# Early sums of the second output projection, angle tables in pieces, and latent value products that alternate between heads

## The reference

```python
mix_out = sliding_window_attention(q, shared_k, shared_v, swa_sinks[bl])
mem_o = memory_attention(mem_q, mem_k, mem_v)
x = x + jnp.concatenate([mix_out, mem_o], axis=-1) @ w_out[layer]
x = x + swiglu(rms_norm(x, ln_ffn[layer]), w_gate_up[layer], w_down[layer])
```

## Time and profile before

| what | value |
| --- | --- |
| median of 3 runs | 2076.44 us (2074.3 to 2078.44) |
| profiled execution, its own time | 2073.64 us |
| its span, from first to last instruction | 2071.8 us |
| TensorE matmul busy | 1925.9 us, 93% |
| VectorE busy | 1059.4 us, 51% |
| ScalarE busy | 780.4 us, 38% |
| mean granted TensorE clock | 0.962 of full speed |

### The profile page before, as it was taken

How to read it: one execution, slowest core, us unless ns; L and a number is a source line. 1 busy time by engine, 2 the same in 40 slices (tenths; PEclk the granted TensorE clock), 3 DMA queues, 4 the chain that set the end, 5 groups by cost and what they waited for, 6 DMA issues and landing times.

```text
span 2071.8 us, 25534 instructions
## 1 busy us (share of the span) xinstructions
PE 1925.9 (93%) x9978; PEld 1498.0 (72%) x9978; DVE 1059.4 (51%) x1979; ACT 780.4 (38%) x1637; POOL 116.5 (6%) x85
## 2 busy tenths in 40 slices
PE   7999988898987769999988999999999899999997
PEld 5665567685554457788887888788876688888886
DVE  6757556441211157785555543644567654444344
ACT  4455744531111145533543321222346543222222
POOL 0000000000000034020420000000000000000000
PEclk9999999999999959999999999999999999999998
DMA  5101413359999942121001222232221022222221
GB/s 190 39 10 53 145 54 112 142 206 405 413 412 408 405 188 72 62 68 65 1 1 59 96 94 102 73 111 97 96 82 41 30 84 102 102 92 92 102 92 41
DMA packets 76791, 261.07 MB, mean 126 GB/s; under 512 B 7776, under 2 KB 10080, under 8 KB 76288
## 3 DMA queue, kind: packets, MB, share of 16 engines
q1 hardware_dynamic: 66512, 231.46, 30.6%
q0 software_dynamic: 5040, 19.58, 2.8%
q10 hardware_dynamic: 5120, 8.39, 1.1%
HBM read 242.62 MB, written 16.79 MB: 125 GB/s over the span
## 4 chain that ended last, share of the span: by engine, by line
PE 72%; DVE 7%; DMA 6%; ACT 3%; issue 1%; POOL 0%; ACTq 0%; DVEq 0%; SPq 0%; POOLq 0%
PE ps_pair L285 17%; PE ps_pair L286 17%; PE ps_pair L287 17%; DMA split_acts_as_f<-w_experts 4%; PE ps_pair L1995 4%; PE ps_turn L2560 2%; PE ps_pair L2560 1%; PE ps_pair L880 1%; PE ps_out L908 1%; DMA w_places<-w_experts 1%; PE ps_shared L2006 1%; PE ps_out L2006 1%; PE ps_turn L892 1%; ACT g L3347 1%; PE ps_out L2326 1%
## 5 line engine op out<-in xcount | busy, mean ns | idle before, releaser
L285 PE MATMUL ps_pair<-split_acts,w_high 128*128 128x512 f32 (+1 forms) x1816 | 721.3, 397 | 22.7 <-DVE split_acts L614 10.0
L287 PE MATMUL ps_pair<-split_acts,w_low 128*128 128x512 f32 (+1 forms) x1816 | 705.3, 388 | 0.0
L286 PE MATMUL ps_pair<-split_acts,w_high 128*128 128x512 f32 (+1 forms) x1800 | 699.2, 388 | 0.0
L242 DVE TENSOR_TENSOR w_low<-w_raw,w_high 128x1024 fp32r<-128x1024 f32 (+4 forms) x249 | 281.9, 1132 | 269.8 <-ACT w_high L236 268.1
L285 PEld LDWEIGHTS ps_pair<-split_acts,w_high 128*128 128x128 f32 x1816 | 343.7, 189 | 103.2 <-issue 23.3
L287 PEld LDWEIGHTS ps_pair<-split_acts,w_low 128*128 128x128 f32 x1816 | 343.6, 189 | 72.0
L286 PEld LDWEIGHTS ps_pair<-split_acts,w_high 128*128 128x128 f32 x1800 | 341.6, 190 | 67.4 <-issue 1.7
L236 ACT ACTIVATE w_high<-w_raw 128x1024 fp32r<-128x1024 f32 (+4 forms) x249 | 242.8, 976 | 147.1 <-PE ps_pair L287 143.2
L360 DVE TENSOR_TENSOR x<-x,ps_pair 128x512 f32<-128x512 f32 x80 | 54.9, 686 | 147.6 <-PE ps_pair L287 147.6
L2237 DVE TENSOR_TENSOR g<-g,ps_pair 64x256 f32<-64x256 f32 x31 | 13.2, 425 | 197.3 <-ACT g L2177 197.3
L3108 ACT ACTIVATE split_acts<-h 128x512 fp32r<-128x512 f32 x44 | 27.8, 633 | 192.4 <-DVE h L3121 192.4
(11 more groups left out here) (528 smaller groups left out, 2453.4 us busy)
## 6 DMA issues: line engine op xcount, KB each, us to landing
w_raw<-w_gu SPq DMA_DIRECT2D x88, 512.0 KB, 3.4
split_acts_as_f<-w_experts SPq DMA_DIRECT2D x42, 1024.0 KB, 21.2
w_places<-w_experts SPq DMA_DIRECT2D x35, 1024.0 KB, 20.6
w_raw<-w_down SPq DMA_DIRECT2D x32, 448.0 KB, 3.2
w_raw<-w_gdnin SPq DMA_DIRECT2D x26, 512.0 KB, 3.5
w_raw<-w_out SPq DMA_DIRECT2D x24, 512.0 KB, 3.5
x<-w_experts SPq DMA_DIRECT2D x12, 1024.0 KB, 20.1
rows_y<-scratch ACTq DMA_DIRECT2D x64, 128.0 KB, 6.1
```

The source lines that it names most:

```text
L242: dve.tensor_tensor(WL[:, t % SPLIT, 0:kt * m], WRAW[:, t % RING, 0:kt * m], WH[:, t % SPLIT, 0:kt * m].bitcast(F32), ALU.subtract).then_i ...
L285: pe.matmul(out, wh[:, k, :], self.high(k), start=(n == 0), stop=False)
L286: pe.matmul(out, wh[:, k, :], self.low(k), start=False, stop=False)
L287: last = pe.matmul(out, wl[:, k, :], self.high(k), start=False, stop=(n == self.kt - 1))
```

## The change

It does three things.

1. `out1.early(j, n0, n1)` issues steps `n0` to `n1` (input tiles in `OUT_ORDER`) of output tile `j` before the stage itself. Tiles 0 and 1 are begun between the gaps 14 to 18: 4 steps of each, then 2 of each, then 1 of each; 7 of 8 steps of both tiles are then done when `out1` begins. It waits for each input tile with `heads_ready`, now for tile 1 too.
2. The work of the two rope tables is spread over tiles 0 to 9 of `gu01` on VectorE, and the two sine functions go to tiles 5 and 11 on ScalarE.
3. `pe_values` of `Attention` issues the value products of the heads that close together in turn: first product of head `h`, first of head `h+1`, second of head `h`, and so on. Each head is reported after its last product. Only the latent attention has groups that close two heads.

```diff
+            def early(self, j, n0, n1):
+
+                def tensor(pe):
+                    self.tensor_steps(pe, j, n0, n1)
+                    self.begun[j] = n1
+                return On(tensor=tensor)
+
             def tensor_tile(self, pe, j):
-                while scores_read:
-                    need(pe, *scores_read.pop())
+                self.tensor_steps(pe, j, self.begun.get(j, 0), self.kt)
+                if j == 0 and self.opening:
+                    self.opening.tensor_spread(pe)
+
+            def tensor_steps(self, pe, j, n0, n1):
                 t = self.base + j
-                pe.wait_ge(low_ready, t + 1)
-                if t >= BANKS:
-                    wait_evac(pe, t - BANKS)
+                if n0 == 0:
+                    while scores_read:
+                        need(pe, *scores_read.pop())
+                    pe.wait_ge(low_ready, t + 1)
+                    if t >= BANKS:
+                        wait_evac(pe, t - BANKS)
...
-                for n, k in enumerate(self.order):
+                for n in range(n0, n1):
+                    k = self.order[n]
                     if j == 0 and self.ready is not None:
                         need(pe, *self.ready(k))
-                    if j == 0 and self.each is not None:
+                    if (j == 0 or j in self.begun) and self.each is not None:
                         self.each(pe, k)
...
-                    rows, plan_ = self.pv(h)
-                    for lhs, (slot, src, q0, q1), first, lastk in plan_:
+                plans = [(h, *self.pv(h)) for h in closes]
+                for n_part in range(len(plans[0][2]) if plans else 0):
+                    for h, rows, plan_ in plans:
+                        lhs, (slot, src, q0, q1), first, lastk = plan_[n_part]
+                        o = self.o0 + h // self.per_tile
                         last = pe.matmul(self.outs[o % len(self.outs)][rows, q0:q1], lhs,
                                          self.turned[h % len(self.turned)][:, slot, src:src + q1 - q0],
                                          start=first, stop=lastk, skip_group_check=True)
-                    done(last, "att_pe", ("values", self.h0 + h))
+                        if n_part == len(plan_) - 1:
+                            done(last, "att_pe", ("values", self.h0 + h))
...
-        swiglu(0, n_ff0, n_kv, hi, lo, {2: [angles_s.part(0)], 8: [angles_s.part(1)]})
+        swa_angles = {0: [On(vector=angles_s.angles)], 6: [On(vector=angles_s.signed)]}
+        for n, at_ in ((0, 1), (1, 7)):
+            for j, step_of in enumerate((angles_s.turned, angles_s.reduced, angles_s.wrapped)):
+                swa_angles[at_ + j] = [On(vector=lambda dve, n=n, step_of=step_of: step_of(dve, n))]
+            swa_angles[at_ + 4] = [On(scalar=lambda act, n=n: angles_s.part_scalar(act, n))]
+        swiglu(0, n_ff0, n_kv, hi, lo, swa_angles)
...
-        fl += [heads.gap(n) for n in range(len(gaps), N_PAIRED + 3)]
...
-        fl += [Linear("out1", hi2, lo2, None, n_ff1.take_act, n_ff1.take_dve, order=OUT_ORDER, each=heads_ready),
-               n_ff1.rest()]
+        out1 = Linear("out1", hi2, lo2, None, n_ff1.take_act, n_ff1.take_dve, order=OUT_ORDER, each=heads_ready)
+        fl += [out1.early(0, 0, 4), heads.gap(14), out1.early(1, 0, 4), heads.gap(15), out1.early(0, 4, 6),
+               heads.gap(16), out1.early(1, 4, 6), heads.gap(17), out1.early(0, 6, 7), out1.early(1, 6, 7),
+               heads.gap(18), out1, n_ff1.rest()]
```

More of the change, by code:

```diff
@@ L260, in __init__ @@
                 self.base = BASE[name]
-                self.order, self.each = order or range(self.kt), each
+                self.order, self.each, self.begun = order or range(self.kt), each, {}
             def tensor(self, pe):
@@ L294, in tensor_tile @@
                             stage.tensor(pe)
-                if j == 0 and self.opening:
-                    self.opening.tensor_spread(pe)
             def scalar(self, act):
```

## The result

The changed kernel takes 2062.89 us (median of 4 runs, 2062.15 to 2064.12); the kernel before, in runs on the same chip, 2075.59 us (4 runs, 2074.3 to 2078.44). The ratio is 0.9934, with an interval of 0.9922 to 0.9945. 2061.0 was predicted, in a range of 2056 to 2068. A further measurement beside 17 runs of the kernel before gave 2062.9 us and 0.9928 (0.9914 to 0.9942). The profiled execution took 2064.12 us, its span is 2062.3. The medians differ by 12.7 us; the ratio makes it 13.7, anywhere from 11.4 to 16.2.

What follows compares the result with a forecast made beforehand. The prediction took TensorE, busy 93% of the span, as the bound. Its terms -3.1 - 5.6 - 6.7 = -15.4 us, made against the median 2076.44, gave 2061.0 us, range 2056 to 2068.

Steps and rivals of the forecast that it cites:

- Angles, -3.1: In `gu01`, spreading the angle work removes two TensorE holes of 1.55 us each: -3.1 us, bounds -2.0 and -3.1.
- Early sums, -6.7: From the last rotation into `out1`, 42 products moved earlier: -6.7 us after a clock allowance, bounds 0 and -8.5.
- so the stage gains 7.5 us: Tail and start of `out1`: 9.5 us of products moved, 2.0 given back, before the clock allowance.
- the 0.8 us set aside for that: At the restart of `out1`: half of the 1.6 us that 8 products at the lower clock would cost.
- The sign of failure that the prediction names for the tail: The prediction is wrong if the last half's values end over 2 us later than before, counted from the last rotation.
- Alternating values, -5.6: At the four latent value pairs, alternating halves run side by side: -5.6 us in all, bounds 0 and -6.3.
- a block becomes 2.29 us: Each latent pair's value block shrinks from 3.86 to 2.29 us, a gain of 1.57 us.
- the allowances for pairs 2 and 3: Latent pairs 2 and 3 gain 1.35 and 1.15 us instead of 1.57, because of VectorE and ScalarE.
- alternation gains nothing: Latent values: the new order brings no gain, leaving -9.8 us in all, 2066.6 us; chance 0.08.
- each product waits for its load: Latent values: 16 weight loads unhidden, block 4.5 us, +2.5 instead of -5.6, in all 2069.1 us; chance 0.03.
- the early products hold up the tail: Tail: early products may add all their 9.5 us there, so that term is 0, in all 2067.7 us; chance 0.08.
- the slower one: From the restart of `out1` the clock stays down, 0.20 us a product, up to +14.6 in all, 2091.0 us; chance 0.02.

Runs made afterwards that it cites:

- early_only: The kernel before with only the early products of the second output projection added; 2068.07 us, ratio 0.9960.
- first12_twice: The kernel before with 12 products of `out1` made ahead of gap 14, thrown away and made again in their place; 2072.72 us, ratio 0.9979.
- values_filled: The kernel before with the alternating value products and 21 throwaway products in TensorE's waits at the latent values; 2069.31 us, ratio 0.9976.
- plain_filled: The kernel before with 21 throwaway products in TensorE's waits at the latent values, value products in their old order; 2073.58 us, ratio 0.9998.
- values_only: The kernel before with only the alternating order of the value products; 2074.78 us, ratio 0.9990.
- first12: The kernel before with only the first 12 products of `out1` moved ahead of gap 14; 2068.92 us, ratio 0.9955.
- tail_cover: The changed kernel with two blocks of early products (12 products) moved from ahead of gaps 17 and 18 to behind gap 18; 2061.11 us, ratio 0.9923.
- before: The kernel before, without any part of the change; 2075.59 us.
- angles_only: The kernel before with only the angle steps in pieces; 2073.71 us, ratio 0.9986.
- before_late40: The kernel before with 40 throwaway products behind the fourth latent value block; 2084.62 us, ratio 1.0039.

## Why the prediction was right, and where a term was off

The direction, the range and the mechanisms of all three parts held; the likeliest time was 1.9 us too low. The gain was 15.4 us in the forecast and 12.7 by the medians, so the sum was 2.7 us too large; 0.85 of these do not show in the time, by luck, because the sum was made from a median of 2076.44 (3 runs) where the kernel before now has 2075.59 (4 runs).

- **Angles, -3.1.** Measured -2.9 alone (0.8 to 5.0 by the ratio) and -3.3 in the trace. The largest piece took 2.80 us as reckoned, and just fits the tile with no idle time to spare. No wait took the place of the two holes.
- **Early sums, -6.7.** The step "so the stage gains 7.5 us" met 7.2 in the trace and -8.5 in the run times of `early_only` (interval -11.2 to -5.4 by its ratio). The full clock in gap 14 was right: scores to the end of the values took 3.1 us, 3.2 were reckoned. The waits at the restart were reckoned at 1.5 and 0.7 us and came as 1.42 and 0.52. The clock did not fall behind them, so the 0.8 us set aside for that was not needed. The sign of failure that the prediction names for the tail, values of the last half more than 2 us later from the last rotation, stayed away: 22.73 us against 22.67, where 0.2 us sooner was reckoned. What the prediction did not separate: `first12_twice` gets 2.5 us from the clock alone, without moving any work out of `out1`. How much of the 7.2 us is the clock's in the full change, whose tail has no low stretch at all, no run separates.
- **Alternating values, -5.6.** This is the term that was mis-sized. The step "a block becomes 2.29 us" held (2.30) wherever the clock was full, and 16 weight loads of 64 columns stayed hidden. By the sentence of "TensorE: Matmul & The Clock Gate", Part 3, The mechanism, of the Trainium skill that the prediction cites, by which a load overlaps products in flight only when the row groups differ, they would have waited; the 2.30 us speak against it. From each block's start to what follows it, `values_filled` gained on `plain_filled` 1.55, 1.10, 0.93 and 1.54, 5.1 us in all, so the allowances for pairs 2 and 3 (1.35 and 1.15) were some 0.5 us too large. The rest went where the prediction had not looked: it allowed for the clock in the tail, where it did not fall, and said nothing of the latent stage, where it does. Against the usual course of the old order, whose fourth block runs partly at the lower clock too, 5.4 of the 5.6 us are there at 285 us; 1.7 are gone by 345, 1.5 of them in the low stretch near 329, and 0.3 more by 1300. The term was thus some 3.4 us by the traces and 1.8 (0.2 to 3.7) by the run times of `values_only`.
- **The profile taken as base.** Its fourth block ran at full clock, where four like ones ran partly at half: up to 1300 us its course is 3.1 to 3.2 us shorter than theirs, about the 2.8 us by which the profiled execution lay below the median. The sum was made against the median, which kept this out of the prediction; profile against profile the alternation looks nearly worthless (-0.3 us).

With the terms as the traces show them, -3.3 - 3.4 - 7.2 = -13.9 us; the run times gave -12.7 by the medians and -13.7 by the ratio, whose interval of 11.4 to 16.2 also holds the 15.4 of the forecast. So it is the traces and not the total that tell the third term from its forecast.

Of the rivals, *alternation gains nothing* and *each product waits for its load* fall by the blocks of 2.30 us; *the early products hold up the tail* by the changed kernel's own tail, 22.73 us against 22.67 with 42 products in it, and by `first12`, whose tail is 2.4 us shorter; the slower one, the clock staying down at the restart of `out1`, by the 1.00 of the stretches. The 4.5 us that the last of these loads would have given did appear, in the fourth block; that it is the clock and not the loads is shown by the three other blocks and by `values_filled`.

## What to carry to other kernels

A change that packs TensorE's work closer, or takes some away, can leave it emptier beside the chains of the other engines, as the shorter blocks did here, so the granted clock is part of its price: look at it in every stretch that the change touches, and in more than one profile. Where TensorE waits for others anyway, put useful work of a later stage there first, as the early sums do; where there is none, throwaway products can pay (by the medians 21 of them made the changed kernel 2.2 us faster, and `tail_cover` 3.6; the same 21 with the values in the old order gave nothing clear). Of the work that can be moved, keep some for the last wait: the order of `tail_cover` is worth 1.8 us with the same instructions.

## What was not expected of the hardware

- Value products of 512, 384, 256 and 128 columns, of two heads in different halves of the output's partitions, run side by side: 16 records with 2560 columns in 2.30 us, the 2.29 of the one head's 8 records.
- The same kernel meets different clocks at the same place from one execution to the next. In the two profiles of the changed kernel the low stretch behind the fourth block lasts 6.8 us (from 276.3 us) and 3.4 us (from 274.3). Kernels that are alike up to the place differ too: with the values in the old order and no fillers, the fourth block took 3.9 us in one profile, 5.6 in four and 6.3 in one. In the tail of the old kernel the lower level lasted 10.2 us in four profiles (`before`, `values_only`, `angles_only` and `before_late40`) and only 3.4 in `plain_filled` and `values_filled`, whose tail is the same. All the runs of the kernel before lie between 2070.4 and 2081.9 us, the ten of the changed kernel between 2061.8 and 2064.1; what narrows them no run shows. The two lines below are of `plain_filled`, whose last rotation is at 1628.82: `out1` starts 20.66 us behind it instead of 22.60.

```profile
1633.18 2.08 PE L3327 MATMUL ps_pair<-g 64*128 64x256 f32 x8 [3.23 <-DVE g L3202]
...
1649.48 0.50 PE L286 MATMUL ps_pair<-split_acts,w_high 128*128 128x512 f32 x1
```
